# A two-mixer trunk: the second mixer's first projection products move into the last tile of the first

## The reference

```
for i in range(DEPTH):                       # 2
    if i % 2 == 0:
        h = h + gla_mixer(rms_norm(h, gla_norm[j]), ...)
    else:
        h = h + gdn_mixer(rms_norm(h, gdn_norm[j]), ...)
...
def gdn_mixer(h, w_in, conv_w, a_log, dt_bias, head_norm, w_out):
    proj = h @ w_in
    qkv, z, beta_logit, a_logit = jnp.split(proj, ...)
    qkv = silu(causal_depthwise_conv(qkv, conv_w))
    ...
    beta = sigmoid(beta_logit)
    log_a = -exp(a_log) * softplus(a_logit + dt_bias)
```

## Time and profile before

| what | value |
|---|---|
| median of three runs | 1576.54 us |
| lowest, highest | 1574.93, 1579.14 us |
| the profiled execution | 1580.03 us |
| its span | 1578.2 us |
| mean granted TensorE clock | 0.969 |
| TensorE busy | 1465.9 us |
| VectorE busy | 786.7 us |
| ScalarE busy | 429.9 us |
| GpSimd busy | 384.5 us |

### The profile page before, as it was taken

One profiled execution on the slowest core, in us unless ns is written; L12 is line 12 of the kernel. 1 busy time (PEld: TensorE's weight loads), 2 busy tenths in 40 slices (PEclk: granted clock), 3 DMA queues, 4 the chain that ended last, 5 costly groups with the idle time before them and its releaser, 6 DMA issues.

```text
span 1578.2 us, 21479 instructions
## 1 busy us (share of the span) xinstructions
PE 1465.9 (93%) x8522; PEld 1233.9 (78%) x8522; DVE 786.7 (50%) x1017; ACT 429.9 (27%) x911; POOL 384.5 (24%) x304
## 2 busy tenths in 40 slices
PE   6999999976999869999999989999999989999997
PEld 5777879964888759999999989988876667777775
DVE  4224412222444417555456799989933444444432
ACT  4415612103222214333432412212221351111111
POOL 3202113315111022222121231222342262222210
PEclk9999999997999979999999999999998989999999
DMA  5421214436654122534446222235355585555520
GB/s 185 150 74 60 88 53 127 148 120 226 201 163 165 71 58 64 129 96 111 128 108 202 76 75 69 81 95 174 107 192 160 180 261 147 161 161 158 156 81 27
DMA packets 206637, 200.81 MB, mean 127 GB/s; under 512 B 62792, under 2 KB 168792, under 8 KB 206288
## 3 DMA queue, kind: packets, MB, share of 16 engines
q1 hardware_dynamic: 199952, 187.99, 39.2%
q10 hardware_dynamic: 6592, 11.54, 2.6%
HBM read 132.39 MB, written 67.09 MB: 126 GB/s over the span
## 4 chain that ended last, share of the span: by engine, by line
PE 43%; DVE 13%; issue 4%; ACT 2%; DMA 1%; SPq 1%; POOL 0%; ACTq 0%; POOLq 0%; DVEq 0%
PE gdn_banks L2390 11%; PE gdn_banks L1726 11%; PE gdn_banks L1672 10%; DVE gdn L1938 6%; PE gdn_banks L2438 2%; PE gdn_banks L2470 2%; PE gdn_banks L2440 2%; DVE gdn L1935 1%; PE gdn_banks L1568 1%; PE gdn_banks L2449 1%; PE gdn_banks L1592 1%; PE gdn_banks L2456 1%; DMA gdn<-gdn_v 1%; DVE gdn L1943 1%; ACT gdn L1797 1%
## 5 line engine op out<-in xcount | busy, mean ns | idle before, releaser
L1672 PE MATMUL gdn_banks<-hn_hi,gdn 128*128 128x344 f32 (+1 forms) x1584 | 323.5, 330 | 2.0 <-POOL gdn L1910 2.0
L1672 PEld LDWEIGHTS gdn_banks<-hn_hi,gdn 128*128 128x128 f32 x1584 | 261.9, 191 | 6.1 <-issue 4.8
L1910 POOL TENSOR_TENSOR gdn<-gdn,gdn 128x1024 fp32r<-128x1024 f32 x33 | 105.8, 3208 | 333.5 <-ACT gdn L1765 333.5
L1672 PE MATMUL gdn_banks<-hn_lo,gdn 128*128 128x344 f32 (+1 forms) x792 | 170.0, 323 | 0.0
L1726 PE MATMUL gdn_banks<-gdn,hn_hi 128*128 128x512 f32 x512 | 164.9, 402 | 0.4 <-DVE gdn L1945 0.4
L1938 DVE SCALAR_TENSOR_TENSOR gdn<-gdn,conv_taps,gdn 128x1040 f32<-128x1040 f32 x96 | 162.2, 1689 | 3.4
L1672 PEld LDWEIGHTS gdn_banks<-hn_lo,gdn 128*128 128x128 f32 x792 | 135.3, 190 | 0.0
L677 PE MATMUL ai_p<-ai_whi,hn_hi 128*128 128x512 f32 x288 | 116.2, 403 | 5.2 <-DVE ai_wlo L528 2.1
L1726 PEld LDWEIGHTS gdn_banks<-gdn,hn_hi 128*128 128x128 f32 x512 | 96.8, 190 | 25.9 <-issue 2.9
L677 PE MATMUL ai_p<-ai_whi,hn_lo 128*128 128x512 f32 x288 | 115.0, 399 | 0.0
L677 PE MATMUL ai_p<-ai_wlo,hn_hi 128*128 128x512 f32 x288 | 114.7, 398 | 0.0
(11 more groups left out here) (286 smaller groups left out, 2620.9 us busy)
## 6 DMA issues: line engine op xcount, KB each, us to landing
gdn<-in_gdn_w_in SPq DMA_DIRECT2D x32, 512.0 KB, 4.1
ai_st<-in_gla_w_in SPq DMA_DIRECT2D x32, 256.0 KB, 4.8
gdn_kq<-gdn SPq DMA_DIRECT2D x16, 512.0 KB, 3.8
gdn_v<-gdn SPq DMA_DIRECT2D x16, 512.0 KB, 3.4
gdn<-in_gdn_w_in SPq DMA_DIRECT2D x32, 256.0 KB, 4.5
gdn<-gdn_kq SPq DMA_DIRECT2D x16, 512.0 KB, 3.5
gdn<-gdn_ek SPq DMA_DIRECT2D x16, 512.0 KB, 5.1
gdn<-gdn_v SPq DMA_DIRECT2D x32, 256.0 KB, 6.0
```

Of the source, the lines that this page charges most:

```text
L1672: last = pe.matmul(a[:, b, 0:m], w[n % 2][:, kt, :], x[:, kt, PAD + s:PAD + s + m], start=(kt == 0 and e == 0), stop=(kt == KT - 1 and e = ...
L1910: pool.tensor_tensor(lo[n % 2][:, :, :], st[n % 2][:, :, :], hi[n % 2][:, :, :].bitcast(F32), ALU.subtract).then_inc(S("ni_wlo"), 1)
```

## The change

A new function `gdn_ahead` lays out the weights of groups 0 and 1 in the part of SBUF where the second mixer keeps them, and gives the pieces that `gla_scan` calls:

- SP, after the load of tile 8's residual: load the weights of group 0 and the two gate slices (`load_weights`; the gate's buffer shrinks from 128 to 40 columns a block). Once tile 8's projection is done, ahead of its last store: convolution taps and small vectors (`load_small`).
- ScalarE and GpSimd, before the last tile's step: the high and low parts of both (`high`, `zero`, `low`).
- TensorE, in `tail`: group 0's first span before the first half of the last output projection, then `norm_out` of tile 7, the second half of the projection, group 0's second span, `norm_out` of tile 8, the gate's first span. 24 products each.
- The last tile no longer computes the state (`outer`, `decs`, `update`), which nothing reads.
- `gdn_in` then makes what is left of group 0 (one span, 24 products) and of the gate (two spans, 48), with the same hooks (`mm_rest`). The loads of groups 2 and 3 go out at once at the start of the block.
- To make room, the tiles of `gla_scan` are placed by hand in one arena, so that the buffers of tile 7 (odd) lie where the new weights go, and all PSUM banks are one tensor that both mixers share. The squares are written to `og` in place of a scratch tile of their own.

```diff
-def over_steps(eng, body, tail):
+def over_steps(eng, body, tail, between=None):
...
     last = NT - 1
+    if between:
+        between()
     body(Step(last, 0, last // 2), True, True)
     tail(Step(last, 0, last // 2))
...
+        low, mid, high_ = A.row(A_DEC), A.row(LATE + KT * P), A.row(LATE + 7200)
...
+        qk = [low.take([P, GH, 3, P]), A.at(LATE + 5664, [P, GH, 3, P])]
+        kx = [low.take([P, GH, C]), high_.take([P, GH, C])]
+        ko = [low.take([P, GH, P]), A.at(LATE + 5152, [P, GH, P])]
+        v = [low.take([P, GH, GDV]), A.at(LATE, [P, GH, GDV])]
+        z = [low.take([P, GH, GDV]), A.at(LATE + 4128, [P, GH, GDV])]
...
-            for t in range(NT - 2, NT):
-                store(Step(t, t % 2, t // 2))
+            sp.wait_ge(S("as_o"), NT - 1)
+            sp.wait_ge(S("as_og"), GH * (NT - 1))
+            H.load_weights(sp)
+            store(Step(NT - 2, 1, (NT - 2) // 2))
+            sp.wait_ge(S("as_y"), 2 * NT)
+            H.load_small(sp)
+            store(Step(NT - 1, 0, (NT - 1) // 2))
...
-                outer(s)
+                if not is_last(s):
+                    outer(s)
...
             def tail(s):
+                H.products(pe, 0, [0])
+                out_project(s, [0])
                 norm_out(s.back(), None)
-                out_project(s)
+                out_project(s, [1])
+                H.products(pe, 0, [1])
                 norm_out(s, None)
+                pe.wait_ge(S("as_su"), GH * (NT - 1))
+                H.products(pe, GATE, [0])
...
-                update(s)
+                if not is_last(s):
+                    update(s)
...
-            over_steps(act, body, tail)
+            over_steps(act, body, tail, lambda: H.high(act))
...
+            def between():
+                pool.wait_ge(S("as_o"), NT - 1)
+                H.zero(pool)
+                H.low(pool)
+            over_steps(pool, body, tail, between)
...
+    def load_weights(sp):
+        sp.dma_start(st[:, :, :], wv[:, :, 0:P]).then_inc(E("gd_w_in"), 16)
+        sp.wait_ge(E("gd_zero"), 1)
+        sp.dma_start(g_st[:, :, 0:NH], wv[:, :, c_gate:c_gate + NH]).then_inc(E("gd_gw_in"), 16)
+        sp.dma_start(g_st[:, :, A0:GW], wv[:, :, c_gate + NH:c_gate + 2 * NH]).then_inc(E("gd_gw_in"), 16)
+
+    def load_small(sp):
+        sp.dma_start(H.cwn, conv_w.rearrange("k (t p) -> t k p", p=P)).then_inc(E("gd_cw_in"), 16)
+        sp.dma_start(H.al[:, :], a_log.rearrange("(h o) -> h o", o=1)).then_inc(E("gd_small_in"), 16)
+        sp.dma_start(H.dt[:, :], dt_bias.rearrange("(h o) -> h o", o=1)).then_inc(E("gd_small_in"), 16)
+        sp.dma_start(H.cm, H.starts_dram[0:NH, :]).then_inc(E("gd_small_in"), 16)
+
+    def high(act):
+        act.wait_ge(E("gd_w_in"), 16)
+        act.activation(hi[:, :, :], st[:, :, :], ACT.Copy).then_inc(E("gd_hi"), 1)
+        act.wait_ge(E("gd_gw_in"), 32)
+        act.activation(g_hi[:, :, :], g_st[:, :, :], ACT.Copy).then_inc(E("gd_hi"), 1)
+
+    def zero(pool):
+        pool.memset(g_st[:, :, :], 0.0).then_inc(E("gd_zero"), 1)
+
+    def low(pool):
+        for n, (l_, s_, h_) in enumerate(((lo, st, hi), (g_lo, g_st, g_hi))):
+            pool.wait_ge(E("gd_hi"), n + 1)
+            pool.tensor_tensor(l_[:, :, :], s_[:, :, :], h_[:, :, :].bitcast(F32), ALU.subtract).then_inc(E("gd_lo"), 1)
...
+    def products(pe, n, spans):
+        pe.wait_ge(E("gd_hi"), n + 1)
+        pe.wait_ge(E("gd_lo"), n + 1)
+        for b in spans:
+            for kt in range(KT):
+                for e in range(3):
+                    product(pe, n, kt, e, b)
...
             t_.then_inc(S("ni_cwT"), 1)
-            for n in range(NIN):
+            mm_rest(0, [2])
+            mm_rest(GATE, [1, 2])
+            for n in range(2, NIN):
                 mm(n)
```

More of the change, by code:

```diff
@@ L806, in split_w_out, with gla_scan @@
     return load, hi, lo
-def gla_scan(nc, S, T, w_out, x, meta, next_norm):
+def gla_scan(nc, S, T, A, H, bank, w_out, x, meta, next_norm):
     with ExitStack() as ctx:
[L811 to L833, removed]
@@ new lines, in gla_scan @@
+        z = [low.take([P, GH, GDV]), A.at(LATE + 4128, [P, GH, GDV])]
+        at = low.take([P, GH, P])
+        sums = low.take([P, 2 * GH + 2])
+        decs = low.take([P, GH, 1])
+        assert low.end <= LATE
+        hres = [mid.take([P, D]), mid.take([P, D])]
+        St = mid.take([P, GH, GDV])
+        assert mid.end <= LATE + 4128
+        og = high_.take([P, GH, GDV])
+        oT_hi = high_.take([P, KT, P], F32R)
+        oT_lo = high_.take([P, KT, P], F32R)
+        hn = high_.take([P, D])
@@ L834, in gla_scan @@
+        nw = high_.take([P, D])
+        assert high_.end <= ARENA
         ss, rs = sums[:, 0:GH], sums[:, GH:2 * GH]
         ss2, rs2 = sums[:, 2 * GH:2 * GH + 1], sums[:, 2 * GH + 1:2 * GH + 2]
[L836 to L841, removed]
+        pO, pU = (bank[:, b:b + 2, :].rearrange("p a (h v) -> p (a h) v", v=GDV) for b in (0, 3))
@@ L842, in gla_scan @@
+        pA, pT = (bank[:, b, :].rearrange("p (h x) -> p h x", x=P) for b in (2, 5))
+        pY = bank[:, 6:8, :]
+        parts = [pT, pA]
         w_load, w_hi, w_lo = split_w_out(nc, S, T, "as", w_out, whi, wlo, [hn[:, :], hres[1][:, :], nw[:, :]])
@@ L845, in gla_scan, with is_last @@
         W_FIRST, W_REST = range(3), range(3, KT)
+        def is_last(s):
+            return isinstance(s.t, int) and s.t == NT - 1
         @block.sync
@@ L1346, in gdn_in @@
         sc_rows = sc[:, 0:2 * C * C].rearrange("p (j w i) -> p j w i", w=2, i=C)
-        al = sb([NH, 1])
+        assert early.end == AL_AT
+        al, dt = H.al, H.dt
+        early.end += 16
         ea = sb([NH, 1])
-        dt = sb([NH, 1])
         junk = sb([P, 4, P])
@@ L1658, in mm @@
             def mm(n):
-                wait(pe, S("ni_whi"), n + 1)
-                wait(pe, S("ni_wlo"), n + 1)
+                pe.wait_ge(S("ni_whi"), n - 1)
+                pe.wait_ge(S("ni_wlo"), n - 1)
                 if n % 2 == 0:
@@ L1676, in mm, with mm_rest @@
                     hooks(n, kt)
-            pe.wait_ge(S("ni_cw_in"), 16)
+            def mm_rest(n, spans):
+                for kt in range(KT):
+                    for e in range(3):
+                        for b in spans:
+                            last = H.product(pe, n, kt, e, b)
+                    if kt == KT - 1:
+                        last.then_inc(S("ni_mm"), 1)
+                    hooks(n, kt)
+            pe.wait_ge(E("gd_cw_in"), 16)
             for k in range(CONV):
```

117 lines of the change are left out of this document (64 added, 53 removed).

## The result

The changed kernel takes 1561.1 us in the median of four executions (1558.92 to 1563.85) against 1576.34 for the kernel before; the ratio is 0.9907 with a 95% interval of 0.9892 to 0.9921, 12 to 17 us. In two later series, again beside the kernel before, it came out at 0.9877 (0.9854 to 0.9901) and 0.989 (0.9871 to 0.9909). The prediction was 1558.6 us in a range of 1553 to 1566, so it held.

The account below looks back on a forecast made before the run. TensorE was taken as busy nearly throughout, gains coming from its waits, with 8.23 us without a product at the seam. 1.55 + 0 + 17.0 + 1.1 - 1.7 = 17.9 us took 1576.54 to 1558.6, range 1553 to 1566.

Parts of the forecast that it names:

- First term: Tail before the barrier: moved products fill TensorE's two holes and the next block starts earlier, 1.55 us gained.
- Second term: Last tile: the new wait of ScalarE and GpSimd for weights is covered by 0.7 to 2.2 us, costing 0.
- rival (d): Last tile: slower, each us of weights landing past 533.9 moves the tail by one, a loss beyond 553; chance 0.02.
- Third term: After the barrier: group 0 ends 4.4 us after the block's start, 17.0 us gained at full clock.
- Fourth term: Gate's products: 48 instead of 72, but q's transposes wait 2.6 us for `silu`, so 1.1 us gained.
- Fifth term: Clock at two new gaps, the barrier and before q's transposes: one fall taken at -1.7 us, bounds 0 and -2.7.
- Rival (a): Gate: early `silu` means q's transposes don't hold TensorE up; 2.6 us more, 22 us gained, about 1554; chance 0.10.
- (b): Last tile: weights or gate slices land late, or the clock falls; gain 10 to 15 us, 1562 to 1567; chance 0.18.
- (c): After the gate: VectorE, busy with convolutions, gives back the early end; gain 5 us or less; chance 0.06.

Follow-up runs that it names:

- the order alone: Kernel before, with only the first half of the last output projection moved ahead of tile 7's transposes: 1573.03 us against 1577.52, ratio 0.9976.
- the late weights: Changed kernel with group 0's weights loaded three times in a row, so that they count as landed later: 1566.49 us, ratio 0.993.
- The later q transposes: Changed kernel with the first head's q transposes and their squares moved behind the gate's group: 1554.56 us, ratio 0.9852.
- changed again: The changed kernel measured and profiled a second time, no edit: 1558.3 us, ratio 0.9877 against the kernel before.
- q transposes later the second time: Repeat of the changed kernel with the first head's q transposes moved behind the gate's group: 1555.32 us, ratio 0.9871.
- third profile: Profile of the changed kernel measured a third time, no edit: 1559.57 us.

## Why the prediction was right

**First term, the tail: 1.55 us forecast, 1.2 measured.** The order rebuilt from the rows came out: 0.72 us of idling before tile 8's transposes (0.8 forecast). The difference is in the barrier: from VectorE's or TensorE's last instruction to the next block it is 1.76 us before and in the run with the order alone, and 2.05 to 2.2 us in the kernels with the rest of the change. Why is not known. But the reading that I gave to this term was wrong. "They fill the two holes" credits the moved products. That is so for the second hole: group 0's second span takes it from 4.46 to 0.72 us at no cost. The first hole is filled for the most part by the projection's first half, which gives 5.2 us alone, and the 72 products together then put the block's start back by 45.8 - 42.1 = 3.7 us. I had costed two edits as one and left the cheaper one unnamed. That the term came out near its size all the same is no luck, as the order was rebuilt whole; only its split between causes was wrong.

**Second term, the last tile's wait: 0 forecast, 0 measured.** Cover forecast 0.7 to 2.2, measured 1.2 in the profile and 1.4 by the late weights. The slower rival (d) priced a late landing at one for one. The gap grew at that price (7.9 us later less 1.2 of cover is 6.7, measured 6.47), but the tail moved by 8.7 us for a gap of 6.5, as the half clock behind it comes on top; and no landing came near the 553 at which it would lose. The weights took 5.4 us to land and the gate's slices 5.0, where the rows of before have 4.6 and 3.8. ScalarE's copy began at 532.8, inside the 531.7 to 533.2, and its copy of the gate's weights followed at once at 533.8. So the small pieces, of which the Trainium skill ("DMA: Bandwidth & Descriptors", Specifications) warns, held nothing up here.

**Third term: 17.0 forecast, (592.55 - 571.07) - (574.58 - 570.15) = 17.0 measured** in the first profile. The 24 products took 3.96 us there, 0.165 us each, so the row's 160 ns held. The 149 ns that the prediction worked out by the Trainium skill ("TensorE: Matmul & The Clock Gate", Back-to-back issue gap) come from a formula that this section gives for an isolated product.

**Fourth term, the gate: 1.1 forecast, 1.0 measured** (11.8 before from group 0's copy to the gate's end, 10.85 after). The gap was 2.70 us for 2.6, ended by `silu`. The later q transposes show that it was on the path.

**Fifth term, the clock: 1.7 forecast, 0 in two profiles of the changed kernel and 4.0 in one.** Here a size was off. With the gap over the barrier at 2.2 us (1.85 forecast), the clock fell in three of seven profiles (changed again, late weights, q transposes later the second time) and stayed in four. Where it fell it cost 6.72 - 3.96 = 2.8 us in two of them and 5.52 - 3.96 = 1.6 us in the late weights, not the 1.7 throughout that I took from the earlier trace rows: I had priced 12 slow products, and all 24 could be. At the q transposes it fell in two of five and cost the 1.0 us forecast in one and 1.2 in the other. Both falls together cost 4.0 us in the second profile, more than the stated bound of 2.7. One fall at 1.7 was a middle value between cases that range from 0 to 4, and that the medians came out near the forecast owes something to this luck.

**The sum.** 19.2 us at the gate's end in the first and third profile of the changed kernel, 15.3 in the second; 15, 18 and 17 us by the medians of three series, against 17.9 forecast. No profile shows anything given back later: behind the gate's end the changed kernel took 969.5 to 977.1 us, the kernel before 973.8, and two of these four profiles, that of before and the third, hold the late spell of low clock. As single profiles scatter by 8 us behind the gate's end, the forecast's own test there, a stretch as long as 973.8 us, could have caught only a large loss. Rival (a) would have needed an earlier `silu`; its 2.6 us became real only with the edit that moves the transposes. Rivals (b), (c) and (d) did not come about.

## What to carry to other kernels

When work is moved ahead of a barrier, rebuild the engine's order up to it and cost each edit on its own: a changed order of what was already there can fill a hole for which the moved work would get the credit. When a stage is shortened, look for the fixed latency of another engine behind it (here copy, convolution and `silu`, 9.2 us), since beyond that length a product saved gave next to nothing here until what waits for it was moved too. And a wait put ahead of an in-order engine's work is free only as far as the engine that needs the result last would have waited anyway. Work that cover out as a number, and test it by making the wait longer.

## What the hardware showed that was not expected

The same gap did not have the same effect. After 2.22 us of idling over the barrier TensorE ran its 24 products at full clock in some executions (3.96 us) and at half in others (6.72 us, granted 0.50), and a gap of 1.67 us before the last tile's scores never cost anything that the profiles show. The spread between executions (1555 to 1565 us for one kernel) is made there only in part: from the gate's end to the end of the span the same code took 969.5, 971.7 and 977.1 us, and 4.7 us of the last are one more fall of the clock, near 1170 us, which 3 of the 12 profiles show in that length. The last idle time of TensorE ahead of it is 1.24 us, and the first profile has 1.26 us in that place and no fall.
